# Expert weight loads in 16 KB runs per partition, in a two-layer hybrid trunk

## The reference, cut to what matters

```python
def expert_choice_ffn(x, w_router, w1, w3, w2):
    cap = EC_FACTOR * T // N_EXPERTS          # 16 of 128 tokens, 32 of 256
    aff = softmax(einsum('btd,de->bte', x, w_router))
    gval, idx = top_k(swapaxes(aff, 1, 2), cap)
    xs = x[idx]                               # per expert, its tokens' rows
    hid = silu(xs @ w1) * (xs @ w3)           # w1, w3: 1024 x 1024 for each of 16 experts
    yo = (hid @ w2) * gval                    # w2: 1024 x 1024
    return scatter_add(idx, yo)

h2 = rmsnorm(x, g_norm2) * (1 + scale2) + shift2
x = x + gate2 * expert_choice_ffn(h2, w_router, w_e1, w_e3, w_e2)
```

## Time and profile before

| | |
|---|---|
| median of 3 runs | 2088.97 us (2087.17 to 2092.86) |
| profiled execution | 2082.25 us, of which the span (first to last instruction) 2080.0 us |
| busy in the span | PE 1892.1 us (91%), DVE 478.8, ACT 355.9, POOL 21.8 |
| read from HBM | 529 MB |
| last `yo` of layer 0, of layer 1 | 1033.61 us, 2066.69 us |

### The profile page before, as it was taken

The page is one execution under the profiler, slowest core; times in us unless marked ns, Lnnn a source line. Parts: engine busy times, 40 slices in busy tenths (PEclk is TensorE's granted clock), DMA queues, the critical chain, the costliest instruction groups (busy, mean ns, idle before and its releaser), DMA issues. The chain is left out here.

```text
span 2080.0 us, 19778 instructions
## 1 busy us (share of the span) xinstructions
PE 1892.1 (91%) x7810; PEld 863.3 (42%) x7810; DVE 478.8 (23%) x1254; ACT 355.9 (17%) x920; POOL 21.8 (1%) x40
## 2 busy tenths in 40 slices
PE   6999999989899988988879999999898999889887
PEld 3464444454534322332235544544545343324322
DVE  1043224353301100100120612254523010001002
ACT  2123222421201000100021231223112010001000
POOL 0000000000000000000000000000000000000000
PEclk8999999989899999999989999999897999999999
DMA  9141113343799999999952312035336999999997
GB/s 373 61 167 66 61 41 121 135 191 121 265 383 410 409 410 410 409 410 410 410 196 81 152 61 85 17 121 203 124 151 256 390 410 409 410 410 409 410 410 281
DMA packets 136067, 532.95 MB, mean 256 GB/s; under 512 B 5120, under 2 KB 5248, under 8 KB 136000
## 3 DMA queue, kind: packets, MB, share of 16 engines
q1 hardware_dynamic: 134448, 527.59, 64.6%
q0 software_dynamic: 1552, 4.44, 0.6%
HBM read 529.13 MB, written 2.88 MB: 256 GB/s over the span
## 5 line engine op out<-in xcount | busy, mean ns | idle before, releaser
L562 PE MATMUL bank<-ring,scr 128*64 128x512 f32 (+1 forms) x2176 | 532.3, 599 | 74.9 <-DMA ring<-in_w_e 57.5
L562 PE MATMUL bank<-ring,hT 128*128 128x512 f32 (+2 forms) x1440 | 597.2, 568 | 2.5 <-DMA ring<-in_w_in 1.3
L562 PE MATMUL bank<-scr 128*64 128x512 f32 (+6 forms) x2048 | 436.9, 520 | 7.9 <-DVE dsm L1720 4.7
L562 PEld LDWEIGHTS bank<-ring,hT 128*128 128x128 f32 x1440 | 268.0, 191 | 270.7 <-issue 264.6
L562 PEld LDWEIGHTS bank<-ring,scr 128*64 128x64 f32 (+1 forms) x2176 | 174.9, 142 | 403.2 <-issue 302.1
L562 PEld LDWEIGHTS bank<-scr 128*64 128x64 f32 (+3 forms) x2048 | 182.7, 164 | 260.6 <-issue 252.2
L1863 DVE TENSOR_TENSOR scr<-scr,bank 128x512 f32<-128x512 f32 x32 | 22.0, 688 | 675.0 <-ACT scr L1378 675.0
L571 PE MATMUL bank<-cst,scr 128*128 128x128 f32 (+1 forms) x530 | 91.4, 288 | 45.9 <-ACT scr L1380 24.9
L1378 ACT ACTIVATE scr<-bank 128x512 f32<-128x512 f32 x32 | 19.1, 597 | 515.1 <-PE bank L562 515.1
L571 PEld LDWEIGHTS bank<-cst,scr 128*128 128x128 f32 (+1 forms) x530 | 58.5, 142 | 109.4 <-issue 77.6
L562 PE MATMUL bank<-ring,csw 128*32 128x512 f32 x384 | 54.6, 708 | 34.7 <-DMA ring<-in_w_ada 19.4
(11 more groups left out here) (206 smaller groups left out, 1018.1 us busy)
## 6 DMA issues: line engine op xcount, KB each, us to landing
ring<-in_w_e SPq DMA_DIRECT2D x124, 2048.0 KB, 21.5
scr<-in_w_e SPq DMA_DIRECT2D x64, 2048.0 KB, 22.2
ring<-in_w_ada SPq DMA_DIRECT2D x24, 2048.0 KB, 10.5
ring<-in_w_in SPq DMA_DIRECT2D x20, 2048.0 KB, 7.9
ring<-in_w_br SPq DMA_DIRECT2D x8, 1024.0 KB, 7.0
ring<-in_w_out SPq DMA_DIRECT2D x4, 2048.0 KB, 8.4
ring<-in_w_in SPq DMA_DIRECT2D x4, 1552.0 KB, 16.7
ring<-in_w_in SPq DMA_DIRECT2D x4, 1536.0 KB, 7.1
```

Source lines behind the costliest of these rows:

```text
L562: ins = pe.matmul(out, lhsT, rhs, start=start, stop=stop, **kw)
```

## The change

It reads an expert half as `(p k) n -> p (k n)`: partition p gets rows 4p to 4p+3 of the half, one run of 16 KB in HBM and in the slot. The chunk k of a half then holds the channels 4n+k (n the partition) of its 512. What is contracted with w1 and w3 must be in that order too:

- `norm_rows` of the second norm writes `xn` permuted (`fours=True`): it reads `x` in steps of four numbers (16 bytes) and writes contiguous rows. Transposes, gathers and `hT` stay as they are. The output order of w1, w3 and w2 is not touched.
- `hid` is stored as before, and its four transposes read every fourth column (`hid[:, :, b]`, stationary operand with steps of 16 bytes), for w2's rows.
- `columns(3)` and `columns(4)` on PE read `rsb` with steps of four numbers (`quads`), 8 products each; those of the first norm do not.
- `wr` is loaded in the new order, and a new tile `cq` holds `g_norm2` and two bias vectors in it. POOL fills `cq` by 24 DMAs per layer, of 32 partitions by 4 numbers, each number a run of its own (4 bytes). They stand last in `parameters`. DVE waits for them (`params_second`) before `columns(3)`.
- Expert 1's eight w1 pieces keep their size and 4 KB runs, with rows four apart.

```diff
         cp = sb("cp", [P, NCOL])
+        cq = sb("cq", [P, 3, KD])
...
-        hid = exp_take(HALF).rearrange("p (b n) -> p b n", b=4)
+        hid = exp_take(HALF).rearrange("p (n b) -> p n b", b=4)
...
+        def quads(ap, k):
+            return ap[:, (k // 4) * HALF:(k // 4 + 1) * HALF].rearrange("p (n b) -> p b n", b=4)[:, k % 4, :]
...
-                    load(base + before, s, (w_e1, w_e3, w_e2)[s // 2][li, e, (s % 2) * HALF:(s % 2 + 1) * HALF, :], D)
+                    w = (w_e1, w_e3, w_e2)[s // 2][li, e, (s % 2) * HALF:(s % 2 + 1) * HALF, :]
+                    if not (isinstance(base + before, int) and base + before == 0):
+                        sp.wait_ge(freed[s], base + before)
+                    sp.dma_start((ring[:, s] if s < SLOTS else more[:, s - SLOTS]).rearrange("p k n -> p (k n)"),
+                                 w.rearrange("(p k) n -> p (k n)", k=4)).then_inc(loaded[s], 16)
...
-                        r = s * HALF + k * P
-                        sp.dma_start(chunk(SLOTS_E + s, k), w_e1[li, 1, r:r + P, :]).then_inc(loaded[SLOTS_E + s], 16)
+                        rows4 = w_e1[li, 1, s * HALF:(s + 1) * HALF, :].rearrange("(p k) n -> k p n", k=4)
+                        sp.dma_start(chunk(SLOTS_E + s, k), rows4[k]).then_inc(loaded[SLOTS_E + s], 16)
...
-                pool.dma_start(wr[:, :, :], w_router[li, :, :].rearrange("(k p) e -> p k e", p=P)).then_inc(params, 16)
+                pool.dma_start(wr.rearrange("p (h b) e -> p h b e", h=2), w_router[li, :, :].rearrange("(h p b) e -> p h b e", h=2, b=4)).then_inc(params, 16)
+                for a in range(4):
+                    for i, c0 in enumerate((COLS["gn2"][0], COLS["bada"][0] + 16, COLS["bada"][0] + 24)):
+                        for h in range(2):
+                            src = colp[li, :, c0 + 4 * h + a].rearrange("(q b) -> q b", b=4)
+                            pool.dma_start(cq[32 * a:32 * a + 32, i, 4 * h:4 * h + 4], src,
+                                           allow_slow_non_contiguous=True).then_inc(params_q, 16)
...
-                        mm(b[:, 2 * k:2 * k + 2], rsb[:, v % 2, k * P:(k + 1) * P], c_("sel"),
+                        mm(b[:, 2 * k:2 * k + 2], quads(rsb[:, v % 2, :], k) if v > 2 else rsb[:, v % 2, k * P:(k + 1) * P], c_("sel"),
...
-                        turn(banks[6][:, b * P:(b + 1) * P], hid[:, b, :], signal=ht_ready if b == 3 else None)
+                        turn(banks[6][:, b * P:(b + 1) * P], hid[:, :, b], signal=ht_ready if b == 3 else None)
...
-            def norm_rows(t0, t1):
+            def norm_rows(t0, t1, fours=False):
...
-                    V.tensor_scalar(xn[:, t, :], x[:, t, :], y, None, ALU.mult).then_inc(xn_ready, 1)
+                    if fours:
+                        V.tensor_scalar(xn[:, t, :].rearrange("p (h b n) -> p h b n", h=2, b=4),
+                                        x[:, t, :].rearrange("p (h n b) -> p h b n", h=2, b=4), y, None, ALU.mult).then_inc(xn_ready, 1)
+                    else:
+                        V.tensor_scalar(xn[:, t, :], x[:, t, :], y, None, ALU.mult).then_inc(xn_ready, 1)
...
+                    if v == 3:
+                        dve.wait_ge(params_q, (li + 1) * 16 * 24)
...
-                    bias = cp[:, COLS["bada"][0] + 8 * n:COLS["bada"][0] + 8 * n + 8]
+                    bias = cp[:, COLS["bada"][0] + 8 * n:COLS["bada"][0] + 8 * n + 8] if v < 2 else cq[:, n - 1, :]
...
-                                               rep(cp[:, 8 * i:8 * i + 8], 2, 2), ALU.add, ALU.mult).then_inc(mod1, 1)
+                                               rep(cp[:, 0:8] if i == 0 else cq[:, 0, :], 2, 2), ALU.add, ALU.mult).then_inc(mod1, 1)
...
-                    V.tensor_tensor(hid.rearrange("p b n -> p (b n)"), hs, banks[7][:, :], ALU.mult).then_inc(hid_ready, 1)
+                    V.tensor_tensor(hid.rearrange("p n b -> p (n b)"), hs, banks[7][:, :], ALU.mult).then_inc(hid_ready, 1)
```

More of the change, by code:

```diff
@@ L313, in trunk_kernel @@
         params = sem("params")
+        params_q = sem("params_second")
         kv_out = sem("kv_out")
@@ L1785, in _ @@
                     if t == 1:
-                        norm_rows(0, 2)
-                norm_rows(2, 3)
+                        norm_rows(0, 2, fours=True)
+                norm_rows(2, 3, fours=True)
                 modulate("h2T", 1)
```

## The result

| | before | after |
|---|---|---|
| median | 2089.51 us (2087.17 to 2092.86, 4 runs) | 2060.28 us (2058.43 to 2063.47, 4 runs) |
| profiled execution, its span | 2082.25, 2080.0 us | 2063.47, 2061.3 us |
| packets of q1 | 134448 | 62256 |
| last `yo` of layer 0 | 1033.61 us | 1027.03 us |

The ratio is 0.9865, 95% interval 0.9853 to 0.9878: 1.35% faster, against 2060.6 us forecast. The two profiled executions lie at opposite ends: that of before is among the shortest of its kernel, that of after the longest of its four. The kernels were timed in four sets of runs, each with the kernel before in it. Where two kernels come from different sets, the difference of their medians carries the scatter of the sets, and their ratios to before are the safer guide.

What follows compares the result with a forecast made beforehand. Loads were taken to bound late experts, PE early ones. Per layer -18 + 2 + 1.6 + 0.2 = -14.2, two layers -28.4, gave 2060.6 us against the median; range 2034 to 2084, 0.8 together.

Steps and rivals of the forecast that it cites:

- What bounds: Experts of both layers: loads pace late experts, PE early ones; faster loads can give at most 67 us.
- cut again: Rival: runs are cut into 4 KB packets again, rate as now, costs stay, +2.7 us a layer, 2094.4; chance 0.08.
- The rate: Expert loads: 16 KB packets raise 410 GB/s to 430, a half taking 4.877 us instead of 5.115.
- All of it: Rival: expert loads reach 443 GB/s with no price on PE, 55 us gained, 2034; chance 0.10.
- half-way: Rival: the load rate rises only to 417 GB/s, 2.7 us a layer gained, 2083.6; chance 0.09.
- HBM: Rival: reads 64 KB apart collide in HBM and the rate falls; at 395 GB/s 2127.6 us; chance 0.07.
- The gain of a layer: Expert loads: 80 halves give 19.0 us, less 1.0 for first halves that can't come sooner: 18 us.
- `hid`, +2 us a layer: Four stepped transpose loads an expert on PE, 0.1 us each, partly hidden where loads pace: +2 us a layer.
- `columns(4)`, +1.6 a layer: Eight products with 16 stepped loads on PE's full path, 0.1 us more each: +1.6 us a layer.
- The norm, +0.2 a layer: DVE's stepped read for `xn` in the second norm, only tile 2 on the path: +0.2, bounds 0 and 0.6.
- The small DMAs, 0: POOL's 24 small DMAs a layer, 13 to 22 us to issue, hidden: nothing, at most 5 us once.
- The announced sign that failed: Profile of the changed kernel: the last `yo` of layer 0 was to come at about 1019.

Runs made afterwards that it cites:

- the kernel with 4 KB packets: The changed kernel with each partition's four rows laid apart in SBUF, so packets end after 4 KB again; same reads in HBM: 2094.08 us, ratio 1.0032.
- whole columns: The changed kernel with ACT writing the rows of columns(3) and columns(4) permuted, so PE reads them contiguously: 2053.83 us, ratio 0.9837; run again 2053.07 us, 0.9824.
- reverse edit: The kernel before with only PE's stepped reads in columns(3) and columns(4) added, output differing from the reference: 2089.46 us, ratio 1.0006.

## Why the prediction came out right

The time was right (2060.28 for 2060.6), and so was the mechanism of the gain: larger packets, a faster stream, late experts at its pace. That it was right to 0.3 us is luck. By the medians gain and costs were each 2.2 us too large, which is also about what the sets scatter, and in the costs one term was much too large (`hid`) while another was missing (the clock).

- **What bounds.** Right. Before and after, late experts go at the pace of the loads, and without the loads' pace the kernel ends 16.7 us a layer earlier. The 67 us put down as the most that loads could give are 33.8 + 31.7 = 65.5 by the runs.
- **A run stays one packet.** Right: 62,256, the number forecast, and *cut again* falls with it. That rival, run as an experiment, gave 2094.08 for its 2094.4.
- **The rate.** 429 GB/s for 430. The slope through the 6144-byte stretch (443) was too steep, as its 2.4 us suggested; the reading by shares, which gave 433, was the better one. The fixed price is 9 ns, not the 15.8 or 11.6 worked out from the earlier trace rows. *All of it*, *half-way* and *HBM* all hang on the rate, and 429 leaves none of them. The new places of the reads in HBM cost nothing that shows: most of the experts' slices stand at 428 or 429.
- **The gain of a layer.** -18 was forecast, and 33.8 / 2 = 16.9 measured by the medians; by the traces of the kernel with 4 KB packets and of the changed one the last `yo` of layer 1 moved from 2080.84 to 2047.97, 16.4 a layer. Most of the miss is the rate: at 429 the 80 halves are worth 409.2 - 391.1 = 18.1 us, where 430 gave 19.0. The 1.0 us taken off for halves that come no sooner was 1.2 to 1.7 by these measurements. By the long stretches it would be more (407 to 423 GB/s is 412.2 - 396.6 = 15.6, so 2.5 us), but a rate in whole GB/s leaves 0.5 us on either side of each. The sign is clear: nine of the fifteen steps from one `yo` to the next in layer 0 of after are PE's own pace (seven of 25.97 us, two with a gather), and there a faster load changes nothing.
- **`hid`, +2 us a layer.** Far too much. It is +0.09 us an expert on PE (0.75 for 0.66, and 25.97 for 25.88 from one early `yo` to the next), so 1.4 a layer at most, if all 16 were paced by PE. I priced every stepped load alike, from the slow `wr` loads. These four aren't slow. That the 128-column product beside each load covers the step is a guess that no run here tests.
- **`columns(4)`, +1.6 a layer.** The loads themselves: right, +1.8. What failed is that a cost was counted as its instructions alone. PE at full clock does 16 loads with two-column products behind them, and when these took 3.7 us the granted clock fell by half, at a cost of 3 us more in the work behind. In the pairs of kernels the whole was worth 7.8 and 1.3 us of two layers, where 3.2 was forecast. The earlier trace rows gave 1.00 and I left the clock there; it had to be looked at where the loads were to become slow.
- **The norm, +0.2 a layer.** 1.13 us for 0.75, and PE's wait went from 1.38 to 1.75 us: +0.4, inside the bounds of 0 and 0.6.
- **The small DMAs, 0.** Right: 13.02 us for 24 issues, as forecast from the earlier trace rows, and nothing when 23 of them go. So is `columns(3)`, hidden in a wait of 4.33 us, of which 2.16 is left. The number of their packets was too high, 216 an engine and layer: q0 rose by 1536 in all, 48 an engine and layer.
- **All costs.** 7.6 us forecast, 5.4 measured at the unchanged rate by the medians, 6.7 by the ratio with an interval from 4.2 to 9.2. That 36 - 7.6 and 33.8 - 5.4 both are 28.4 is luck. The second is 2088.71 - 2060.28, across two sets; in its own set the change gave 29.2. The local prices don't add up to the measured costs either: twice 1.8 + 3 for `columns(4)`, 0.4 for the norm and about 1 for `hid` would be some 12 us. Trace against trace it is nearer to that: the span with 4 KB packets is 2094.2 us and that of the kernel before in its second trace 2085.1, 9.1 apart, with the clock low for 145 and 132 us. So the costs are known to some 3 us only.
- **The announced sign that failed.** The last `yo` of layer 0 at 1027.03, not 1019. 14.2 us earlier than 1033.61 was meant against the profiled execution, which was a short one. Before again had its last copy at 1036.90, and the changed kernel in a later set at 1024.77: 12.1 us earlier, where 14.2 was forecast.

The version with whole columns, 2053.07 us, beats both kernels: 0.9824 of before, for the change of one write on ACT beside the new read on PE.

## What to carry to other kernels

Where a stream of loads has no gap and PE waits for it, look at the bytes per packet before anything else: here 4 KB runs ran at 410 GB/s, 8 KB at 422 and 16 KB at 429. About two thirds of that rise, and 25.7 of the 33.8 us, are already in the step to 8 KB. Pay for the new order of rows with an engine that writes the data anyway and stands off the path, not with PE's reads. A stepped stationary read was cheap where 128-column products stand beside it and dear where the products have two columns, and there it can cost more in the work right behind it, through the clock, than in itself (3 us for 1.8). Before a price of a few us is believed, look at the granted clock over the whole span of both executions.

## What the hardware showed that was not expected

- A stationary read in steps of 16 bytes doubles the time of a narrow product: 3.66 / 16 = 0.229 us for 1.84 / 16 = 0.115, with two columns. The clock isn't the reason: `columns(3)` of the reverse edit took 3.89 us for 1.95 with the clock at 1.00 throughout. With 128 columns it is 0.75 / 4 = 0.19 for 0.66 / 4 = 0.165. The Trainium skill, "Advanced Engine Details and Errata", section "SBUF Cachelines", says that two hits on a 16-byte line are needed for full pace; the first pair agrees that a read below that is slow, by a factor of two here, and in the second pair the loss is small, which that rule doesn't say.
- The granted clock fell to 0.50 out of full work: PE had no idle time between 467.85 and 480.79, and then only slow weight loads and two-column products. It was so in both layers of eight traces.
- Executions of one kernel differ in how long the clock stands at its lower level (the kernel before: 121 us of one, 132 of the other), and their spans with it (2080.0 and 2085.1).
- A packet has a price of about 9 ns at every size between 4 and 16 KB, with the bytes at 37.6 ns per KB on top.
